# A hybrid decoder step on one core: three phases in a row, or one pipeline over token tiles

## The reference

```
h = rms_norm(x); z = h @ w_in          # 1024 -> 8704: q, k, v 1536 each, GLU 2048, gates 2048
A = silu(layer_norm(causal_conv31(a * sigmoid(g)))) @ w_conv_proj
B = attention(q, k, v) @ w_attn_proj   # 3 groups x 8 heads x 64; window/dilation 128/1, 512/4, 2048/16
x1 = x + (sig(gA) * A + sig(gB) * B) @ w_out
h2 = rms_norm(x1); q = h2 @ w_peer_q   # 8 retrieval heads, 2 halves of 128
s1, s2 = q halves x 128 sub keys; top 16 each; top 16 of the 256 sums; g = softmax
idx = e1 * 128 + e2                    # 8 x 16 = 128 experts of 16384 per token
y = x1 + sum_k g_k * gelu(h2 . expert_u[idx_k]) * expert_v[idx_k]
```

## Time and profile before

| | |
|---|---|
| median of 3 runs | 2526.94 us (2526.22 to 2531.91) |
| span of the profiled execution | 2533.2 us |
| PE, DVE, ACT, POOL busy | 86%, 66%, 32%, 32% |
| moved | 699.53 MB |
| first gather starts | 1011 us |

### The profile page before, as it was taken

How to read it: one execution, slowest core, us unless ns; L and a number is a source line. 1 busy time by engine, 2 the same in 40 slices (tenths; PEclk the granted TensorE clock), 3 DMA queues, 4 the chain that set the end, 5 groups by cost and what they waited for, 6 DMA issues and landing times.

```text
span 2533.2 us, 23227 instructions
## 1 busy us (share of the span) xinstructions
PE 2189.8 (86%) x6924; PEld 1124.0 (44%) x6924; DVE 1663.0 (66%) x3796; ACT 802.1 (32%) x2246; POOL 809.7 (32%) x736
## 2 busy tenths in 40 slices
PE   6999999998988997878877888878888878888877
PEld 3554466664644445444442344433344423334321
DVE  2187866776568613789786458885477874487854
ACT  1001031212431100444444334443344443344432
POOL 0002122233342200333434444343443343343342
PEclk9889999998888998899999999999999999999999
DMA  4212211225557345889899999999999999999998
GB/s 133 67 38 81 77 48 68 79 103 190 184 173 274 97 143 208 318 320 383 348 374 420 375 413 372 363 381 405 385 404 360 367 417 368 410 374 377 381 413 354
DMA packets 139040, 699.53 MB, mean 276 GB/s; under 512 B 15113, under 2 KB 23305, under 8 KB 67236
## 3 DMA queue, kind: packets, MB, share of 16 engines
q0 software_dynamic: 83600, 586.52, 58.6%
q1 hardware_dynamic: 55316, 111.53, 12.8%
HBM read 683.46 MB, written 14.11 MB: 275 GB/s over the span
## 4 chain that ended last, share of the span: by engine, by line
PE 25%; DMA 18%; DVE 9%; ACT 5%; issue 4%; POOL 1%; POOLq 0%; DVEq 0%
DMA p_ring<-in_expert_uv,p_idx 18%; PE p_acc L1657 17%; PE p_q L1622 4%; PE p_o L1600 3%; DVE p_ring L1847 2%; ACT L1722 2%; ACT p_diag L1726 1%; ACT p_wgt L1724 1%; POOL p_ring L1586 1%; ACT L1704 1%; DVE p_ti L1775 1%; DVE p_ti L1778 1%; DVE p_sco L1776 1%; ACT p_gel L1722 1%; PE p_k L1632 1%
## 5 line engine op out<-in xcount | busy, mean ns | idle before, releaser
L1657 PE MATMUL p_acc<-p_ring,p_diag 128*128 128x512 f32 (+1 forms) x2176 | 1067.8, 632 | 264.1 <-ACT p_diag L1726 250.7
L1847 DVE CUSTOM_DVE_ANT_0 p_ring<-p_ring,yT 128x1024 f32<-128x1024 f32 x544 | 660.2, 1225 | 407.3 <-DMA p_ring<-in_expert_uv,p_idx 399.6
L1586 POOL DMA_INDIRECT p_ring<-in_expert_uv,p_idx x544 | 604.5, 1111 | 922.1 <-PE p_acc L1657 852.3
L1657 PEld LDWEIGHTS p_acc<-p_ring,p_diag 128*128 128x128 f32 (+1 forms) x2176 | 395.8, 194 | 856.9 <-issue 855.7
L1722 ACT ACTIVATE p_gel<-p_dots 128x1 f32<-128x1 f32 x544 | 109.0, 200 | 702.2 <-DVE p_dots L1847 693.7
L460 PE MATMUL f_z<-wring,hT 128*128 128x512 f32 (+1 forms) x608 | 270.6, 600 | 0.0
L1726 ACT ACTIVATE p_diag<-cst,p_wgt 128x128 f32<-128x128 f32 (+1 forms) x544 | 215.9, 397 | 17.7
L460 PEld LDWEIGHTS f_z<-wring,hT 128*128 128x128 f32 (+1 forms) x608 | 149.1, 250 | 103.9 <-issue 61.4
L697 DVE SCALAR_TENSOR_TENSOR yT<-f_uT,f_vec,yT 128x512 f32<-128x512 f32 x240 | 179.0, 746 | 6.9 <-PE f_a L464 3.6
L1622 PEld LDWEIGHTS p_q<-hT,p_wq 128*128 128x128 f32 x1280 | 156.7, 194 | 36.8 <-issue 34.8
L1724 ACT ACTIVATE p_wgt<-p_gel,p_gw 128x1 f32<-128x1 f32 x544 | 160.4, 295 | 17.7
(11 more groups left out here) (277 smaller groups left out, 2125.4 us busy)
## 6 DMA issues: line engine op xcount, KB each, us to landing
wring<-in_w_in SPq DMA_DIRECT2D x13, 2048.0 KB, 8.4
qk<-x_q SPq DMA_DIRECT2D x16, 1024.0 KB, 7.8
qk<-in_cache_kv_g SPq DMA_DIRECT2D x10, 1024.0 KB, 5.9
p_ring<-in_expert_uv,p_idx POOLq DMA_INDIRECT x544, 9.1
wring<-in_w_in SPq DMA_DIRECT2D x8, 1024.0 KB, 10.4
p_wq<-in_w_peer_q SPq DMA_DIRECT2D x4, 2048.0 KB, 16.3
m_vr<-in_cache_kv_g SPq DMA_DIRECT2D x6, 1024.0 KB, 7.9
qk<-in_cache_kv_g SPq DMA_DIRECT2D x20, 256.0 KB, 5.5
```

Of the source, the lines that this page charges most:

```text
L1586: eng.indirect_dma_start(ring[:, t % RING, :], None, a["expert_uv"], bass.IndirectOffsetOnAxis(col, 0)).then_inc(row_in[t % RING], 16)
L1657: mm = eng.matmul(acc[h][0:n, :], diag[:, t % 4, 0:n], ring[:, t % RING, D + 512 * h:D + 512 * (h + 1)], start=(k == 0), stop=(t == end_of ...
L1847: eng.tensor_tensor_reduce(u, u, h2[:, tile % 2, :], 1.0, 0.0, ALU.mult, ALU.add, dots[:, t % 4:t % 4 + 1]).then_inc(dot_ready, 1)
```

## The change

The program is written anew as one pipeline. The unit of work is a token tile (four prompt tiles of 128, then the 32 sample tokens). For each tile the whole layer up to the retrieval scores is one run of `TICKS`; the gather steps of the preceding tile are laid between.

- **Weights.** Each tile streams all of them, 30 units per tile (4 GLU, 12 q/k/v of 384 columns, 4 gates, 2 conv projection, 2 attention projection, 2 `w_out`, 4 `w_peer_q`), 54.5 MB. The host lays them out so that each partition reads one piece of 8, 12 or 16 KB. In tile 0 five buffers are used (three of them are the ring of the gathers); after that two, and a unit's load is started when the unit two before it is done.
- **PE.** All projections have the tokens stationary and 384 or 512 weight columns moving. A tick is two such matmuls and what `plan()` puts there (transposes, scores, LayerNorm sums). `step_marks()` spreads the gather steps over the ticks in proportion to a table of PE costs: 0 in tile 0, 112 in tile 1, 128 in each of tiles 2, 3 and 4, and 48 after the last tick.
- **Attention** keeps the tokens in natural order and masks the dilated groups: tiles 0 to 3 have 3, 6, 8, 10 blocks per head, 27 in place of 15. Keys and values of earlier tiles go through memory (`x_kh`, `x_vh`). Sample attention runs as matmuls over caches laid out by the host.
- **Convolution.** Four of eight channel groups on DVE (128 tokens per instruction), four on POOL, two instructions of 128x512 per tap (L853, L854).
- **Gather steps.** A step now holds two experts for 64 tokens, the rows of `h2` come from memory into `rep`, and the weights are folded by a 128x64 matrix. There are again 544 steps of 1.05 MB. Scores, indices and weights pass through memory or small transfers (`sco2`, `pick`: 128 transfers of 64 x 2 x 8 elements).

The core of the diff (the file is replaced as a whole):

```diff
-def front(nc, a, sc, cst, yT, hT, wsb, w_in, qk, S, trig_d):
-def middle(nc, a, sc, cst, yT, hT, mT, wring, w_in, qk, S, late):
-def peer(nc, a, cst, yT, mT, wo, late):
...
-            for t in range(STEPS):
...
-                if t >= RING:
-                    eng.wait_ge(v_used, t - RING + 1)
-                col = idx[:, tile % 2, k:k + 1] if tile < NT else idx4[:, k:k + 1]
-                eng.indirect_dma_start(ring[:, t % RING, :], None, a["expert_uv"], bass.IndirectOffsetOnAxis(col, 0)).then_inc(row_in[t % RING], 16)
...
+RING = 6
+LEAD_V, LEAD_A = 2, 2
+def step_marks():
+    marks = []
+    for t in range(NT + 1):
+        some = [n for n in range(len(TICKS)) if tick_tile(n) == t]
+        cost = np.array([sum(map(pe_cost, TICKS[n])) + 0.1 for n in some])
+        if t == 1:
+            cost[:12] = 0.0
+        cost = np.cumsum(cost)
+        lo, hi = (0, 0) if t == 0 else (0 if t == 1 else P * (t - 1) - 16, P * t - 16)
+        marks += [lo + int((hi - lo) * c / cost[-1] + 1e-9) for c in cost]
+    return marks
...
+            def load(u):
+                if BUF_BEFORE[u] is not None:
+                    eng.wait_ge(z_ready, BUF_BEFORE[u] + 1)
+                eng.dma_start(buffer(u), a["w_" + kind][n]).then_inc(w_in[BUF[u]], 16)
...
+        @block.gpsimd
+            for n, tick in enumerate(TICKS):
+                if n >= ENDS[0]:
+                    steps_upto(MARK[n - 1] + RING)
...
+                    link(eng.tensor_tensor(ctm[:, :, :], win, w, ALU.mult))
+                    ins = eng.tensor_tensor(out, out, ctm[:, :, :], ALU.add)
...
+        @block.tensor
+            for n, tick in enumerate(TICKS):
+                for v in tick:
+                    if v[0] == "mm":
+                        multiply(*v[1:])
...
+                steps_upto(MARK[n])
...
+        @block.vector
+                    conv_upto(t, conv_at(n, CONV_V * TAPS))
+                steps_upto(lead(n, LEAD_V))
```

More of the change, by code:

```diff
@@ L33 @@
 AW = NG * GW
+HP = HG // 2
+QW = NG * P
 TAPS = 31
@@ new lines, in rounds, with blocks_of, runs @@
+def rounds(t):
+    g1 = [(1, u) for u in range(t + 1)]
+    g2 = [(2, t)] + [(2, u) for u in range(t)]
+    g0 = [(0, u) for u in (t - 1, t) if u >= 0]
+    if t == 3:
+        return [(0, g1), (6, g2), (4, g0)]
+    return [(3 - t, g1 + g0[:-1]), (5, g0[-1:] + g2)]
+def blocks_of(t):
+    return [b for _, some in rounds(t) for b in some]
+def runs(some):
+    out = []
+    for at, (g, u) in enumerate(some):
+        if out and out[-1][1] == g and out[-1][2] + out[-1][3] == u:
+            out[-1][3] += 1
+        else:
+            out.append([at, g, u, 1])
+    return out
@@ new lines, with conv_at, item_marks @@
+BUF, BUF_BEFORE, BUF_NTH = unit_buffers()
+RING_FREE = max(u for u in range(len(UNITS)) if BUF[u] >= 2)
+QK = [s for s in UNITS if s[0] == "qkv" and s[3] < 2]
+QK_NO = {s[1:]: e for e, s in enumerate(QK)}
+CONV_V, CONV_P = 4, 4
+def conv_at(n, total):
+    t = tick_tile(n)
+    first, last = ENDS["conv", t]
+    return min(total, max(0, -(-total * (n - first + 1) // (last - first + 1))))
+def item_marks():
+    at = []
+    for t, h in ITEMS:
+        if t == 0:
+            at.append(-1 if h < 2 else 8 * (h - 2))
+        elif t == NT:
+            at.append(P * NT - 16 + 4 * h)
+        else:
+            at.append(P * t - 16 + 4 * h if h < 4 else P * t + 8 * (h - 4))
+    return at
@@ L298, in front, with sems @@
[L298 to L302 removed]
+            return ctx.enter_context(nc.semaphore(name))
+        def sems(name, n):
+            return [sem(f"{name}{j}") for j in range(n)]
+        cst = sb("cst", [P, C_W])
+        ring = sb("ring", [P, RING, 2 * D])
+        wts = sb("wts", [P, 2, DC * 512])
+        rep = sb("rep", [P, 2, D])
@@ new lines, in _, with steps_upto @@
+            done = [0]
+            def steps_upto(last):
+                for t in range(done[0], last):
+                    g, k = group_no(t)
+                    tile, j = GROUPS[g]
+                    n = GRP if tile < NT else SMP
+                    if k == 0 and g:
+                        eng.wait_ge(y_ready, g)
+                    eng.wait_ge(fold_ready, t + 1)
+                    for h in range(2):
+                        mm = eng.matmul(acc[h][GRP * h:GRP * h + n, :], fold[:, t % 4, 0:n], ring[:, t % RING, D + 512 * h:D + 512 * (h + 1)],
+                                        start=(k == 0), stop=(k == GSTEPS[g] - 1))
+                    mm.then_inc(v_used, 1)
+                done[0] = max(done[0], last)
```

2889 lines of the change are left out of this document (1334 added, 1555 removed).

## The result

The changed kernel takes 2769.6 us (2768.3 to 2770.5, four runs), the kernel before 2528.8 us on the same chip (2526.2 to 2531.9): a ratio of 1.096, 95% interval 1.094 to 1.098. The forecast was 2690 us, with a range of 2470 to 2880. The profiled span is 2767.9 us, 235 us over that of before.

The account below looks back on a forecast made before the run. PE and DMA were both wanted for nearly the whole of each stage. Tile 0 283, larger of both 2014, norms 48, weight loads 32, DVE/POOL 105, remainder 40, tail 172: 2694, forecast 2690 us, range 2470 to 2880.

Parts of the forecast that it names:

- The sum of 2694 us: Whole kernel: tile 0, the larger of PE and DMA per stage, and five extras, held against the profiled span of 2533 us.
- PE work: Four overlapped stages: projections, attention and gather steps need 452, 492, 502 and 568 us of PE at a clock of 0.95.
- The step of 1.72 us: PE's price for one gather step, at 0.857 us per 512-wide matmul, steps and projections alike.
- Bytes: Four overlapped stages: 187, 206, 206 and 226 MB at 420 GB/s, 445, 490, 490 and 538 us of DMA.
- DVE and POOL: q/k/v part: two-operand DVE instructions stand still while POOL's run; 35 us in each of three prompt stages, 105 us.
- Rival 3: q/k/v part: POOL, DVE and PE go in turns, 65 us more per prompt stage; 2800 to 2960 us, chance 0.17.
- Weight loads: After the half-sized `ap` units: 4 us of waiting for each of two loads per tile, 32 us (0 to 80).
- Norm chains: Later tiles: norms at `x` and `h2` stand in a chain on PE's queue, 12 us per tile, 48 us.
- Remainder of 2%: In-order waits: PE follows DVE and ACT with two steps of lead, POOL issues by PE's progress; 40 us (0 to 150).
- A sign of being wrong: Profile after: the forecast is wrong if a single wait, such as PE on weights, makes over 150 us.
- Tail: Last 48 steps: retrieval items of the sample tile make DVE need 3.7 us in 32 of them; 172 us.

Follow-up runs that it names:

- experiment 2: Changed kernel with thin weight loads (512 columns per unit, tiles 1 to 4): 2604.5 us; with GpSimd's taps 1 to 30 one token wide: 2620.3; both: 2438.3.
- experiment 4: The 91 us: run with all three edits, but convolution split as in the changed kernel and taps 1 to 30 of both engines one token wide: 2545.5 us.
- all three edits: Changed kernel with early norm and early score fetch, steps weighed 1.4 times in the q/k/v part, and the whole prompt convolution on DVE: 2636.7 us.
- both thinned: Changed kernel with weight units of tiles 1 to 4 cut to 512 columns and GpSimd's taps 1 to 30 one token wide: 2438.3 us, ratio 0.967.
- experiment 1: Changed kernel with the folding matrix 128 columns wide, so each matmul of a prompt step writes all 128 partitions: 2827.8 us, ratio 1.120.

## Why the prediction was right in its time and not in its reasons

The sum of 2694 us for the span met 2768: 74 us short, 3%. Errors in both directions met in it, so a part of this closeness is luck. By its steps:

- **PE work: wrong.** The step of 1.72 us was read from matmuls of 128 columns and given to matmuls of 64. It is 1.08 us at full clock, or 1.2 with what the projection behind it loses (2.92 us less the 1.72 of four records). I had written down the fold by a 128x64 matrix and not asked what its shape does to the price. The Trainium skill, "TensorEngine Tiling (Array Packing)", section Key Properties, says that tiles of the array operate independently and can execute weight loads and matmuls in parallel. The trace agrees: 1.08 us for a pair of halves, 1.88 for a pair of full width, and the records of halves start 7 ns apart. The forecast's PE terms of 452 to 568 us met 409, 434 and 448 busy in the prompt stages and 427 in the sample stage. The clock was 0.85 to 0.88 and not 0.95, which hides how much less work it is. PE was to be 85 to 92% busy in the four stages and was 73 to 77%.
- **Bytes: right.** 928 MB for about 920, and 409 GB/s over 280 us for the 420 assumed. That PE was struck out as a bound hardly moved the floor, since the byte terms lay within 30 us of PE's in each stage: 1963 instead of 2014 us. By the figure of the Trainium skill ("DMA: Bandwidth & Descriptors", Specifications, about 358 GB/s) the estimate for the whole was 2760 us, and the result is 2770. That is chance: the 409 GB/s over 280 us say that 358 GB/s is no limit here.
- **DVE and POOL: right mechanism, right place, size and scope short.** The forecast had 105 us in three prompt stages; experiment 2 gives 114 there. It left out tile 0, where the same taps run and nothing else covers them: 40 us, as much as the difference between 283 and 320. The instruction's own maximum is 1996 ns, 1.65 us over its median; I had expected 1.1 (L1411). For the dot product, 2328 against 1224 ns, 1.1 is right.
- **Rival 3: half of it happened.** Its condition, DVE with all of POOL's blocking over PE's work in the q/k/v part, was met: 223 us of DVE against 179 of PE in 240. What it gave for that, 65 us instead of 35 per prompt stage, is too much against 27 to 46.
- **Weight loads: mis-sized.** 32 us, where PE waited 74 us for weights in the four stages (26.7 of them for `cp` units, 8.1 for `ap`); how much of that the time would give back wasn't tried.
- **Norm chains: mis-sized.** 12 us per tile, where PE waited 77 us at four boundaries for the norm alone (the 106.4 us of L1065 less 29.5 at the start). The missing link was a round trip of the scores through memory on DVE's queue ahead of the norm. Moving both gave 51 us back, about the 48 of the whole term.
- **Remainder of 2%, 40 us: too small, and the step I trusted least.** I put it down mainly to the bounds taking turns: while DVE binds, the DMA engines are at 85%, and the reverse. Moving steps gave 27 us, a seventh slot 20 at most. What else is in it isn't shown.
- **A sign of being wrong that was met.** A single wait was to stay under 150 us. PE waited 208 us for ACT's folding matrix, and DVE 586 for rows. The first is no bound by itself: with longer leads it fell by 124 us and the time rose.
- **Tail: right**, 168 us for 172, with DVE busy for 137 of them, where the sum had 32 x 3.7 + 16 x 1.31 = 139 us of its work.

So a term too large (PE, which made 51 us of floor) and some that were too small (tile 0, weight loads, boundary, turns) met in the sum. The direction rested on bytes and on DVE, and that held: a gather step with all that lies beside it costs 4.6 us (2280 us of the four stages over their 496 steps) instead of 2.77.

**Where the expected gain went.** Some 700 us of front work lie under the gathers now. Paid for it were, by the runs: the part of the weights of four more tiles that experiment 2 took away (165 us), GpSimd's half of the convolution with its blocking (149), and the boundaries (51). That is 365 us of the some 940 between a gain of 700 and a loss of 241. The 91 us of experiment 4 don't come on top, since they hold the half that DVE had taken over; no run splits the rest. In the kernel before the mixer's work was done once for 512 tokens, with 512-wide instructions on DVE and one pass over the weights.

**What stays open.** Tile 4 and the tail took 752 us in the changed kernel, 756 with all three edits and 718 with both thinned. No run was aimed at them. There DMA is 92% busy until 2600 us and DVE 81% after it; whether the caches or the retrieval of 32 rows hold it wasn't tried. Nor was a convolution on PE.

## What to carry to other kernels

- Two resources can bind a pipeline stage between them although neither is busy all of it (here DVE 63 to 67% and the DMA engines 88 to 91% of a prompt stage), if their loads lie in different parts. Cut a stage into its parts before taking the larger of two sums, and spread movable work by the engine that binds in each part, not by one engine's cost table: ten of 128 steps moved gave 27 us here.
- When one in-order queue waits for a round trip through memory, list what stands behind it on that engine, and then what stands behind that on the next. Here the norm moved alone gave 16 us, and the norm and the fetch 51.
- A longer lead between engines isn't slack: with a ring of fixed size it takes away from the time that a transfer has. Count steps from a slot's release to the first wait for it.

## What the runs showed of the hardware

- Two matmuls with a stationary operand of 64 columns, written to partitions 0 to 63 and 64 to 127 of two banks, take 1.08 us together and start 7 ns apart; with 128 columns 1.88 us.
- Taking turns between them and matmuls of 128 columns costs some of this: a step and four records of a projection take 2.92 us from start to start with narrow steps and 3.44 with wide ones, so 0.5 us are spared.
- Beside GpSimd's instructions with two SBUF operands a DVE instruction of the same kind took up to 1.65 us longer (0.44 us at most without them), and one of 128 columns, 0.35 us by itself, 0.57 in the mean. 480 beside GpSimd took 248.7 us and 960 alone 265.8.
- Less work on PE lowered its granted clock: 0.849 of full speed with narrow steps, 0.911 with wide ones, for the same projections. By the estimate of experiment 1 some 43 us of the time that narrow steps saved were given back by the clock in one group of projections.
- The DMA engines held 409 GB/s for 280 us with gathers of 8 KB rows, weights, and small index pieces mixed.
